# Experts through slots in DRAM: token rows scattered, outputs fetched by indirect transfers, and factor transposes in the block inverse

## What is computed

```python
# GDN: per head and chunk
lmat = jnp.where(strict, einsum(k_beta, k) * decay, 0.0)
t_inv = triangular_solve(eye + lmat, eye, lower=True, unit_diagonal=True)
...
# experts (TOP_K = 2 of N_EXPERTS = 8, hidden width 1408)
logits = xt @ w_router + b_router
top_v, top_i = lax.top_k(logits, 2)
gates = softmax(top_v)
y = sum over e of dense_gate[:, e] * ((silu(xt @ w1[e]) * (xt @ w3[e])) @ w2[e])
x = layer_norm(ALPHA * x + y)
```

## Time and profile before

| | us |
|---|---|
| median of the runs shown (3: 1516.19 to 1519.16) | 1516.45 |
| the profiled execution's own time | 1511.28 |
| its span, from the first to the last instruction | 1509.5 |
| PE busy | 1411.4 (94%) |
| DVE busy | 429.2 (28%) |
| ACT busy | 255.4 (17%) |
| POOL busy | 157.2 (10%) |
| DMA, mean over the span | 180 GB/s |

### The profile page before, as it was taken

The page is one execution under the profiler, slowest core; times in us unless marked ns, Lnnn a source line. Parts: engine busy times, 40 slices in busy tenths (PEclk is TensorE's granted clock), DMA queues, the critical chain, the costliest instruction groups (busy, mean ns, idle before and its releaser), DMA issues.

```text
span 1509.5 us, 24400 instructions
## 1 busy us (share of the span) xinstructions
PE 1411.4 (94%) x10741; PEld 946.2 (63%) x10741; DVE 429.2 (28%) x929; ACT 255.4 (17%) x576; POOL 157.2 (10%) x121
## 2 busy tenths in 40 slices
PE   7998999899999979985999999999995979999998
PEld 6888996677777758434545554555553744766673
DVE  1626644242253065133111110211124061000001
ACT  2442022121010012420111111112121021100000
POOL 1020000406666000000000000000006000000000
PEclk9999999899999989995999999999997999999999
DMA  8414010835433744745899899889568050334430
GB/s 310 164 56 140 1 57 0 245 105 167 139 116 132 93 150 102 304 156 179 309 345 332 329 367 317 326 334 375 177 240 227 0 223 0 112 123 156 167 112 28
DMA packets 103068, 272.33 MB, mean 180 GB/s; under 512 B 5628, under 2 KB 37472, under 8 KB 103008
## 3 DMA queue, kind: packets, MB, share of 16 engines
q1 hardware_dynamic: 98128, 259.93, 49.7%
q0 software_dynamic: 3792, 11.00, 2.9%
q10 hardware_dynamic: 1088, 0.52, 0.2%
HBM read 269.34 MB, written 2.10 MB: 180 GB/s over the span
## 4 chain that ended last, share of the span: by engine, by line
PE 89%; DVE 7%; ACT 2%; issue 1%; DMA 0%; POOL 0%; DVEq 0%; POOLq 0%
PE bank L1503 25%; PE bank L1938 15%; PE bank L1971 8%; PE bank L2077 7%; PE bank L1510 6%; PE bank L1781 5%; PE bank L1886 4%; PE bank L1481 3%; PE bank L1913 2%; PE bank L1812 2%; PE bank L1636 2%; PE bank L1638 1%; PE bank L1948 1%; PE bank L1760 1%; PE bank L1834 1%
## 5 line engine op out<-in xcount | busy, mean ns | idle before, releaser
L1503 PE MATMUL bank<-xT,arena 128*128 128x256 f32 x1856 | 415.2, 384 | 4.2 <-issue 1.4
L1503 PEld LDWEIGHTS bank<-xT,arena 128*128 128x128 f32 x1856 | 354.5, 192 | 61.9 <-issue 9.0
L1938 PE MATMUL bank<-arena 128*32 128x352 f32 x3072 | 228.7, 459 | 1.0 <-DVE arena L1087 1.0
L1938 PEld LDWEIGHTS bank<-arena 128*32 128x32 f32 x3072 | 100.2, 110 | 126.6 <-issue 125.4
L1971 PE MATMUL bank<-arena 128*32 128x256 f32 x2112 | 115.6, 379 | 0.0
L2077 PE MATMUL bank<-arena 128*128 128x512 f32 x256 | 111.0, 592 | 0.0
L1971 PEld LDWEIGHTS bank<-arena 128*32 128x32 f32 x2112 | 67.8, 110 | 45.1
L2077 PEld LDWEIGHTS bank<-arena 128*128 128x128 f32 x256 | 48.6, 190 | 58.2 <-issue 57.9
L1781 PE MATMUL bank<-arena 128*128 128x512 f32 x176 | 77.5, 594 | 0.0
L1110 DVE TENSOR_TENSOR arena<-arena,bank 128x352 f32<-128x352 f32 x24 | 12.5, 522 | 196.5 <-PE bank L1938 196.5
L1481 PE MATMUL bank<-const,arena 128*128 128x128 f32 x288 | 41.8, 288 | 26.0 <-DVE arena L1131 19.2
(11 more groups left out here) (338 smaller groups left out, 1461.9 us busy)
## 6 DMA issues: line engine op xcount, KB each, us to landing
arena<-moe_w SPq DMA_DIRECT2D x64, 1408.0 KB, 9.1
arena<-ffn_w SPq DMA_DIRECT2D x33, 1024.0 KB, 7.8
arena<-moe_w SPq DMA_DIRECT2D x32, 1024.0 KB, 7.4
arena<-gdn_w_in SPq DMA_DIRECT2D x8, 2048.0 KB, 9.7
arena<-w_up SPq DMA_DIRECT2D x8, 2048.0 KB, 8.2
arena<-w_down SPq DMA_DIRECT2D x8, 2048.0 KB, 8.0
arena<-moe_w SPq DMA_DIRECT2D x24, 384.0 KB, 7.5
arena<-s_w_glu SPq DMA_DIRECT2D x4, 2048.0 KB, 11.0
```

Of the source, the lines that this page charges most:

```text
L1503: last = mm(bank[:, at:at + SEQ], w[:, k, P * m:P * m + P], x[:, k, :], start=(k == 0), stop=(k == KT - 1))
L1938: last = mm(banks[i][32 * q:32 * q + 32, 0:EW1], xg[:, EK * s + kk, 32 * t:32 * t + 32], w[:, kk, EW1 * q:EW1 * q + EW1], start=(s == 0 an ...
```

## The change

**Inverse.** D is no longer updated by a product. `level_turn` transposes the updated DT back (four transposes a group), and ScalarE, which has nothing else to do there, copies them to D. The D products and VectorE's subtraction go. The transposes of group j stand behind P of group j + 1, those of group 3 behind Q of the next level's group 0.

**Slots.** A DRAM tensor `slot_rows` of 25 x 96 rows of 1024 (three passes of eight experts and one spare) is filled with zeros once: GpSimd's kzero now covers 128 partitions, and ScalarE issues one DMA behind the SiLU of FFN tile 1, after waiting for `kz_stored`. SyncE's table loads and ScalarE's first `take_w` wait for it too.

**Routing.** Both halves of the logits go to one bank and are handled by one set of operations. The comparison comes first, so `chosen` is signalled before maxima and gates. The first expert's tokens are still gathered by one-hot products, made right after `place`. Only after that VectorE computes each token's two slot rows (`token_rows`, int32) and its two gates (`gate_of`). GpSimd scatters xres to the slots of both its experts by four indirect DMAs, multiplies xres by ALPHA, and waits for the loop.

**A turn.** ScalarE loads the next expert's 96 rows to `xrow`; TensorE transposes them (eight transposes) where the gather stood, into banks 0 and 1. The spread products, the gate transposes, the one-hot matrices, macc and its sums are gone. The down-products go by block t inside each chunk, and block t only waits for its own hidden rows. Outputs are copied as [128, 256] per block (two by ScalarE, one by VectorE), and ScalarE stores them with four DMAs to the expert's slots, whose token rows have been read by then.

**After the loop.** While the last expert runs, GpSimd fetches each token's output from the lower-numbered of its two experts by two indirect DMAs, scales them with its gate and adds them to xres. After the last store it fetches the other output; LayerNorm's first operation multiplies that by its gate and adds it.

```diff
+            slot_rows = slots.rearrange("a s d -> (a s) d")
+            pool.wait_ge(xrow_loaded, 16)
+            pool.wait_ge(routed, 2)
+            for i in range(2 * NT):
+                pool.indirect_dma_start(slot_rows, bass.IndirectOffsetOnAxis(ap=token_rows[:, i:i + 1], axis=0), xres[:, i % NT], None).then_inc(rows_moved, 16)
+            pool.wait_ge(passes_ready, 1)
...
+            for n in range(NT):
+                link(nc.gpsimd.tensor_scalar(xres[:, n], xres[:, n], ALPHA, None, ALU.mult))
+            pool.wait_ge(y_stored, n_pass * (64 * EXPERTS))
...
+            for n in range(NT):
+                pool.indirect_dma_start(y_first[:, n], None, slot_rows, bass.IndirectOffsetOnAxis(ap=token_rows[:, NT + n:NT + n + 1], axis=0)).then_inc(rows_moved, 16)
+            pool.wait_ge(rows_moved, 96)
+            for n in range(NT):
+                link(nc.gpsimd.tensor_scalar(y_first[:, n], y_first[:, n], gate_of[:, 1, n:n + 1], None, ALU.mult))
+                nc.gpsimd.tensor_tensor(xres[:, n], xres[:, n], y_first[:, n], ALU.add).then_inc(x_mixed, 1)
+            pool.wait_ge(m_y, n_pass * (EXPERTS * (EC + 2)))
+            pool.wait_ge(y_stored, n_pass * (64 * EXPERTS) + 64)
+            link(nc.gpsimd.tensor_tensor(pool_pad, zero_c, zero_c, ALU.add))
+            for n in range(NT):
+                pool.indirect_dma_start(y_last[:, n], None, slot_rows, bass.IndirectOffsetOnAxis(ap=token_rows[:, n:n + 1], axis=0)).then_inc(y_fetched[n], 16)
...
 # VectorE, LayerNorm's first operation after the experts
+                        y, by = src(n, hf)
+                        link(V_.scalar_tensor_tensor(r, y, by, r, ALU.mult, ALU.add))
 # VectorE, routing
+            dve.wait_ge(route_done, 1)
+            link(V_.tensor_tensor(logits, banks[0][:, 0:16].rearrange("p (n e) -> p n e", n=NT), over(router_b, NT), ALU.add))
...
+            V_.tensor_scalar(chosen, rank, 2.0, None, ALU.is_lt).then_inc(chosen_ready, 1)
...
+            link(V_.memset(mh, 0.0))
+            dve.wait_ge(place_done, 1)
...
+                last = V_.tensor_scalar(pick[:, n], mat(C_IOTA)[:, 0:SLOTS], 1.0, place[:, n, 0:1], ALU.add, ALU.is_equal)
+            last.then_inc(routed, 1)
...
+            take_tokens(0, banks[6], banks[7])
...
+            V_.tensor_copy(token_rows[:, :], rows_f.rearrange("p a b -> p (a b)")).then_inc(routed, 1)
 # VectorE, a turn
-                picks(pick, k + 1, False, pick_ready)
...
-                add_scattered(k * 4, 0)
-                take_tokens(k + 1)
-                add_scattered(k * 4, 1)
...
+                take_tokens(k + 1, banks[0], banks[1])
+                dve.wait_ge(y_stored, k * 64 + 64)
+                dve.wait_ge(m_y, k * (EC + 2) + EC + 1)
+                V_.tensor_copy(ysb[:, 1], banks[7][:, 0:EW2]).then_inc(m_yread_v, 1)
 # ScalarE, inverse, first FFN, a turn
+            for i in range(4 * (LEVELS - 2)):
+                j = i % 4
+                act.wait_ge(d_tr, 5 + i)
+                nc.scalar.copy(D[:, 4 * j:4 * j + 4], four(banks[4 + j % 2])).then_inc(d_evac, 1)
...
+                if m == S5_FIRST - 2:
+                    act.wait_ge(kz_stored, 64)
+                    act.dma_start(slots.rearrange("a s d -> s a d"),
+                                  kzero[0:SLOTS, None, :].broadcast_to((SLOTS, MAX_PASS * EXPERTS + 1, DM))).then_inc(xrow_loaded, 16)
...
+            act.wait_ge(rows_moved, 64)
             with act.Fori(0, n_pass * EXPERTS) as k:
+                act.wait_ge(gath_done, k * 2 + 2)
+                act.dma_start(xrow, slots[bass.ds(k + 1, 1)].rearrange("a s d -> (a s) d")).then_inc(xrow_loaded, 16)
...
+                act.wait_ge(m_yread_a, k * 2 + 4)
+                act.wait_ge(m_yread_v, k + 2)
+                for q in range(EC):
+                    act.dma_start(slots[bass.ds(k, 1), :, EW2 * q:EW2 * q + EW2].rearrange("a (t i) d -> i (a t) d", i=32),
+                                  ysb[32 * q:32 * q + 32]).then_inc(y_stored, 16)
 # TensorE
-                    if lv < LEVELS - 1:
-                        last = mm(four(banks[4 + j % 2])[:, b % 4], QT[:, b], D[:, b], start=True, stop=True)
...
+            def level_turn(lv, j):
+                i = 4 * (lv - 1) + j
+                pe.wait_ge(lv_pe, i + 1)
+                if i >= 2:
+                    pe.wait_ge(d_evac, 4 + i - 1)
+                for b in range(4 * j, 4 * j + 4):
+                    last = transpose(four(banks[4 + j % 2])[:, b % 4], DT[:, b])
+                last.then_inc(d_tr, 1)
...
                 hidden(0)
                 hidden(1)
-                gather(k + 1)
+                pe.wait_ge(xrow_loaded, k * 16 + 32)
+                for i in range(2):
+                    for c in range(4):
+                        last = transpose(banks[i][:, SLOTS * c:SLOTS * c + SLOTS], xrow[:, P * (4 * i + c):P * (4 * i + c) + P])
+                    last.then_inc(gath_done, 1)
                 pe.wait_ge(m_h, k * ST + 3)
                 hidden(2)
...
+                    for t in range(ST):
+                        if c == 0:
+                            pe.wait_ge(m_hT, k * ST + t + 1)
+                        for b, m in ((0, c), (1, EC + c), (2, 2 * EC + c)):
```

More of the change, by code:

```diff
@@ L111, in build @@
         norm_w = sb("norm_w", [P, 2, DM])
[L112 removed]
+        small = sb("small", [P, 896])
         arena = sb("arena", [P, 44288])
@@ L1054, in _ @@
-            link(V_.memset(place, -1.0))
-            link(V_.memset(gates, 0.0))
-            for t in range(MAX_PASS):
-                last = V_.tensor_copy(gates[:, :, EXPERTS * t:EXPERTS * t + EXPERTS], gate)
-            last.then_inc(chosen_ready, 1)
-            dve.wait_ge(place_done, 1)
-            for n in range(NT):
-                link(V_.tensor_tensor(place[:, n, 0:EXPERTS], banks[n][:, 0:EXPERTS], chosen[:, n], ALU.mult))
-            for t in range(1, MAX_PASS):
-                link(V_.tensor_scalar(place[:, :, EXPERTS * t:EXPERTS * t + EXPERTS], place[:, :, 0:EXPERTS], -1.0 - SLOTS * t, None, ALU.add))
@@ new lines, in _ @@
+            V_.tensor_tensor(cmp_b, other, mine, ALU.is_gt)
+            link(V_.tensor_tensor(cmp_a, other, mine, ALU.is_equal))
+            link(V_.tensor_tensor(cmp_a, cmp_a, tri, ALU.mult))
+            link(V_.tensor_tensor(cmp_a, cmp_a, cmp_b, ALU.add))
+            link(V_.tensor_reduce(rank, cmp_a, AX, ALU.add))
+            V_.tensor_scalar(chosen, rank, 2.0, None, ALU.is_lt).then_inc(chosen_ready, 1)
+            for n in range(NT):
+                last = V_.max(top[:, n], logits[:, n])
@@ new lines, in _ @@
+            link(last)
+            V_.tensor_tensor(etop[:, :, 0:1], top[:, :, 1:2], top[:, :, 0:1], ALU.subtract)
+            V_.tensor_tensor(gate, logits, top[:, :, 0:1].broadcast_to((P, NT, 8)), ALU.subtract).then_inc(route_read, 1)
+            link(V_.memset(mh, 0.0))
+            dve.wait_ge(place_done, 1)
+            dve.wait_ge(chosen_ready, 1)
+            link(V_.tensor_tensor(place, banks[1][:, 0:16].rearrange("p (n e) -> p n e", n=NT), chosen, ALU.mult))
+            for n in range(NT):
+                last = V_.tensor_scalar(pick[:, n], mat(C_IOTA)[:, 0:SLOTS], 1.0, place[:, n, 0:1], ALU.add, ALU.is_equal)
@@ L1095, in _, with take_tokens @@
-            dve.wait_ge(passes_ready, 1)
-            link(V_.memset(macc, 0.0))
-            link(V_.memset(mh, 0.0))
-            link(V_.memset(ysb, 0.0))
-            link(V_.memset(spread, 0.0))
-            picks(pick, 0, False, pick_ready)
-            picks(pick_g, 0, True, pickg_ready)
-            take_tokens(0)
+            def take_tokens(k, first, second):
+                for i, bank in ((0, first), (1, second)):
+                    dve.wait_ge(gath_done, k * 2 + i + 1)
+                    V_.tensor_copy(xg[:, 4 * i:4 * i + 4].rearrange("p a b -> p (a b)"), bank[:, 0:4 * SLOTS]).then_inc(xg_ready, 1)
@@ L1943, in _ @@
                         last.then_inc(m_slab, 1)
-                pe.wait_ge(m_yread_a, k * ST + 3)
-                pe.wait_ge(m_yread_v, k * ST + 3)
-                pe.wait_ge(m_h, k * ST + 1)
-                for hf in range(2):
-                    mm(banks[hf][:, :], spread[:, 0], ysb[:, 512 * hf:512 * hf + 512], start=True, stop=True).then_inc(m_sc, 1)
                 pe.wait_ge(m_h, k * ST + 2)
@@ L1975, in _ @@
-            pe.wait_ge(m_yread_v, n_pass * (EXPERTS * ST) + ST)
-            pe.wait_ge(m_spr, n_pass * EXPERTS + 1)
-            for n in range(NT):
-                for hf in range(2):
-                    pe.wait_ge(m_acc, n_pass * (EXPERTS * 4) + 2 * n + hf + 3)
-                    mm(banks[hf][:, :], spread[:, n], ysb[:, 512 * hf:512 * hf + 512], start=True, stop=True).then_inc(m_sc, 1)
+                        if c == EC - 1 or t == ST - 1:
+                            last.then_inc(m_y, 1)
```

216 lines of the change are left out of this document (93 added, 123 removed).

## The result

The changed kernel took 1472.42 us (median of four runs, 1464.07 to 1481.22), the kernel before beside it 1516.32 us (1515.97 to 1519.16): a ratio of 0.9719, 95% interval 0.9695 to 0.9744. The forecast was 1446 with a range to 1468, so the change saved 44 us of the 70 expected. The profiled execution of after took 1464.07 us, span 1462.2; its span is 47.3 us shorter than that of before.

The account below looks back on a forecast made before the run. TensorE was taken to bound the kernel, with DMA next and near. Terms -53.4 + 2 - 11.2 - 11.7 + 4 + 0 = -70.3 us took 1516.45 to 1446; range 1436 to 1458, to 1468 with rival 1.

Parts of the forecast that it names:

- The turn, on DMA: Expert loop: added row load and store make the DMA cycle 49.3 us against turns of 44.7, costing +2 us.
- the step's own formula: Expert loop: 19.6 + 6 x cycle may reach 312.9, when expert 7's first slab is due; the cycle limit is 48.9 us.
- rival 1: Expert loop: DMA becomes the bound; at a cycle of 52.2 us the time is 1464, slow tail included; chance 0.16.
- The turn, on TensorE: Expert loop: spread products, gather and gate transposes go, turns fall from 51.4 to 44.7 us; eight save 53.4 us.
- The inverse: Inverse: transposes replace the D products, levels fall from 11.17 to 8.9 us; five levels save 11.2 us.
- rival 4: Inverse: transposes let the clock fall to 1.2 GHz, its 50 us double, giving 1496 us; chance 0.03.
- The routing: Router to first up-product: fewer linked operations and an earlier gather bring the first up-product to 700.4, saving 11.7 us.
- The zero fill: First FFN, ScalarE's queue: issue held a few us inside 19 us of room, cost 0; +6 if held to the end.
- rivals 2 and 3: First FFN: zero fill holds ScalarE until it drains, 1487 us, chance 0.08; or below 110 GB/s, slower, 1525, chance 0.04.
- The tail: After the expert loop: stores and indirect fetch delay LayerNorm, costing +4 us, with ends +1 and +12.
- D + 15: Tail: LayerNorm's forecast start, 15 us after the eighth turn's end (D), against D + 10.8 before the change.

Follow-up runs that it names:

- the late loads: The changed kernel with SyncE loading the dense MLP's later bulk weights only after the expert outputs are fetched: 1462.48 us, ratio 0.9652.
- the two sets of runs: The changed kernel measured twice, unchanged, each time beside the kernel before: 1472.42 us, ratio 0.9719, and once more 1470.39 us, ratio 0.9711.
- its two variants: The kernel before with only the inverse's part of the change, 1501.97 us; and with each quarter's third down-projection weight block as one 128-row load, 1514.98 us.
- blocks by VectorE: The changed kernel with hidden columns dealt out so VectorE transposes the hidden blocks and down-projection weights load as whole 128-row blocks: 1439.33 us, ratio 0.9492.
- one load: The changed kernel with each quarter's third down-projection weight block as one load of 128 rows instead of 96 and 32: 1446.09 us, ratio 0.9545.
- both together: The changed kernel with VectorE transposing the hidden blocks, whole 128-row weight blocks, and bulk loads after the fetch of expert outputs: 1426.77 us, ratio 0.9426.

## Why the prediction was wrong

**The turn, on DMA** is the step that failed. Its mechanism was right: the next bound, the buffer slack, waits that begin late in the loop. The size was off: +2 us at a cycle of 49.3; the measured cycle is 50.7, and the last three turns are 16.3 us longer than 44.58 each (by 4.4, 6.1 and 5.7). By the step's own formula, 19.6 + 6 x 50.7 - 312.9 = 10.9. Of the rest, 2.3 us come from the refills, which began 9.4 us into the first turn and not 7.1: they begin 7.6 us into a turn when nothing holds TensorE, and in its first slab TensorE lost time around 699 us, at a granted clock of 1.00, for a reason that the trace doesn't show. Another 1.7 are the up-products behind the last wait (192 instructions), which took 16.10 instead of 14.38 us, with the clock at 0.66 between 1033 and 1038. Some 1.4 us stay open. The formula gives 6 us for each us of cycle above 48.9. I took the lower end of a term of 2.0 to 4.9 us (measured: 50.7 - 47.3 = 3.4), which put the cycle 0.4 above that limit, where the result hangs on a size that the rows didn't fix.

What makes the cycle long is shown: with the third blocks whole it is 44.6 us or less, and the waits are gone. The forecast's 47.3 us already had these slow loads in them, since they were measured with them. Why the added row traffic then cost 3.4 us instead of 2.0 is open: in the kernel before the queues moved 336/0.92 = 365 GB/s while busy, by which 18.1 MB are an estimated 49.6 us, and in the last three turns of after, full all the time, they moved 356.

What I missed is that one rate doesn't hold for all loads. The 387 GB/s of the stretch 730 to 740 was a stretch of slab loads, and I put it against rival 1. The trace of before shows two rates in one turn, slabs first, then the blocks of the down-projection, at the same share:

```profile
790.00:795.00 5.00, 5.00 (x43) 2.65 (x36) 2.19 (x4) 1.20 (x4) 0.00 (x0) 1.00 1.01 421
...
810.00:815.00 5.00, 5.00 (x100) 3.03 (x96) 0.00 (x0) 0.00 (x0) 0.00 (x0) 1.00 1.01 315
815.00:820.00 5.00, 5.00 (x76) 2.18 (x69) 2.98 (x8) 3.46 (x7) 0.00 (x0) 1.00 1.02 318
```

A share of 1.0 at 318 GB/s beside one of 1.0 at 421 says that some loads fill the queues with less than they could carry. With the third blocks whole, the kernel before moved the down-projection's blocks at 365 and 351 GB/s at shares of 0.90 and 0.93 in the same two stretches. The Trainium skill (HBM Reference, Specifications (TRN2)) has some 358 GB/s as a core's share when both cores of a pair load, and some 425 for a core alone, which is this kernel's case. The 358, which I set aside, gave an estimated 50.5 us and +10, nearer than my term; yet not for its reason, since the same bytes went at 406 once the loads were whole.

The others, by their steps. **The turn, on TensorE**: 44.7 forecast, 44.58 measured. **The inverse**: levels of 8.9 forecast and 8.89 measured, -11.2 against -11.4; the clock stood at 1.00, with 1.8 us of transposes in each level of 8.89, and rival 4 did not come. **The routing**: -11.7 against -11.9. Bias sum to first up-product took 12.3 us (12.5 forecast). **The zero fill**: 0 against 0; its issue took 0.41 us, so there was not even the hold of some us, and rivals 2 and 3 fall. **The tail**: +4 forecast, +6.0 measured; the first LayerNorm operation came 16.6 us after the last product, against D + 15. Bulk loads beside the row transfers are the price, as the late loads show. **Not in the sum** were 8.2 us, nearly all of them clock: 3.5 in the input stage, which differ between executions, and 4.7 behind the tail. The forecast watched the clock in the inverse alone.

So 70.3 forecast, and 14.5 (loop) + 2.0 (tail) + 8.2 (not in the sum) - 1.7 (the other stages) = 23.0 missing in the profiled execution: 47.3. Rival 1 gave 1464, which that execution took, the fastest of its four; the medians of the two sets of runs are 1470 and 1472. The rival was said to have the slow tail in it: with +12 instead of +4 there its price is 1472, and the range should have gone that far instead of ending at 1468.

With whole loads the kernel takes 1446.09 us. That this is the forecast's number is partly luck. By stage that execution is 65.4 us shorter than the profiled one of before, not 70.3: 22.4 up to the loop (22.9 forecast), 53.3 in the loop (51.4), then 7.3 lost in the tail (4 forecast) and 3.0 behind it (none). The other 5 us are that the profiled execution of before ran 5.2 below its median. It had the clock at 1.00 between 90 and 100 us, where the profiles of its two variants had 0.66.

## What to carry to other kernels

Read the DMA view as share and GB/s together, for each kind of load by itself: a full share at a low rate means loads of a bad form, which cost nothing under a long turn and set the pace once the turn is shorter. A load should fall evenly on both halves of the partitions, 0 to 63 and 64 to 127; if rows must be split, split them by even and odd, or by columns. A small transfer on the path that ends a stage wants the bulk loads behind it to start after it.

## What the runs showed of the hardware

- Of two loads of 64 rows each, lower and upper half made the kernel 1482.01 us, even and odd partitions 1447.58, and two of 512 columns on all partitions 1447.19.
- The 16 DMA engines together moved 406 to 408 GB/s over some 220 us, reads and row traffic together, while the share read 1.02; at 356 it read 1.03.
- Four stores of 96 KB landed in 3.3 us from their issue without bulk beside them and in 7.8 us with it; an indirect fetch of 128 rows costs GpSimd 0.96 to 1.05 us of issue.
- The clock behind the tail is not set by the length of the wait ahead of it: the same 32 products took 15.97, 15.76 and 15.73 us after waits of 32.07 (after), 24.83 (late bulk loads) and 33.37 us (blocks by VectorE), and 13.97 us after waits of 33.35 (one load) and 24.85 us (both together).
